# Two value products in a row: latent attention with its products done for a pair of items in every other step

## The reference, cut to what matters

```python
def _block_attention(q, k, v):          # 8 heads, 512 queries, 768 keys (256 context + 512 latent)
    ...
    def one(qi):                        # a block of 128 queries
        s = jnp.einsum('bqhd,bkhd->bhqk', qi, k, preferred_element_type=jnp.float32) * scale
        p = jax.nn.softmax(s, axis=-1).astype(v.dtype)
        return jnp.einsum('bhqk,bkhd->bqhd', p, v)
```

## Time and profile before

| | |
|---|---|
| median of 3 runs | 2680.9 us |
| profiled execution, time | 2680.16 us |
| its span | 2678.4 us |
| TensorE busy | 2626.2 us, 98% |
| VectorE busy | 1157.1 us, 43% |
| ScalarE busy | 924.9 us, 35% |
| the stretch of the 32 items, from the span's start | 472 to 577.4 us |
| TensorE busy from 490 to 570 us | 80.00 of 80 us |

### The profile page before, as it was taken

How to read it: one execution, slowest core, us unless ns; L and a number is a source line. 1 busy time by engine, 2 the same in 40 slices (tenths; PEclk the granted TensorE clock), 3 DMA queues, 4 the chain that set the end, 5 groups by cost and what they waited for, 6 DMA issues and landing times.

```text
span 2678.4 us, 34877 instructions
## 1 busy us (share of the span) xinstructions
PE 2626.2 (98%) x14767; PEld 2154.1 (80%) x14767; DVE 1157.1 (43%) x1737; ACT 924.9 (35%) x1401; POOL 157.4 (6%) x268
## 2 busy tenths in 40 slices
PE   7999999999999999999999999999999999999998
PEld 5888887678888888867888888888888776888887
DVE  3414653666333243567433324333234467533322
ACT  3222333643222234455322223222224456322211
POOL 0140000001000001111000000000000010100000
PEclk9999999999999999999999999999999999999999
DMA  9631241012333332211233332333233212232221
GB/s 296 211 128 48 64 126 40 33 56 79 95 94 96 108 100 79 64 48 64 95 95 96 105 113 66 125 95 95 94 95 99 64 48 80 71 95 95 94 96 78
DMA packets 213953, 249.12 MB, mean 93 GB/s; under 512 B 12880, under 2 KB 193703, under 8 KB 213799
## 3 DMA queue, kind: packets, MB, share of 16 engines
q1 hardware_dynamic: 213798, 246.90, 28.9%
HBM read 244.78 MB, written 2.10 MB: 92 GB/s over the span
## 4 chain that ended last, share of the span: by engine, by line
PE 92%; DVE 3%; ACT 2%; issue 1%; POOL 1%; DMA 0%; SPq 0%; DVEq 0%; POOLq 0%; ACTq 0%
PE psum L751 89%; PE psum L1293 1%; PE psum L1209 1%; PE psum L821 1%; DMA mod_w<-in_ab_w_mod 0%; DVE stats_first L2021 0%; DVE work L2014 0%; DVE w_lo L1934 0%; ACT w_hi L1467 0%; POOL stats_first L2604 0%; DVE X L2017 0%; ACT work L1508 0%; ACT log_weights L1485 0%; POOL stats L2659 0%; DVE wide L2047 0%
## 5 line engine op out<-in xcount | busy, mean ns | idle before, releaser
L751 PE MATMUL psum<-h_hi,w_hi 128*128 128x512 f32 (+1 forms) x2096 | 782.7, 373 | 0.6 <-DVE w_lo L1934 0.3
L751 PE MATMUL psum<-h_lo,w_hi 128*128 128x512 f32 (+1 forms) x2096 | 775.6, 370 | 0.0
L751 PE MATMUL psum<-h_hi,w_lo 128*128 128x512 f32 (+1 forms) x2096 | 775.5, 370 | 0.0
L1934 DVE TENSOR_TENSOR w_lo<-raw,w_hi 128x2048 fp32r<-128x2048 f32 (+1 forms) x174 | 396.8, 2283 | 695.7 <-ACT w_hi L1467 695.6
L751 PEld LDWEIGHTS psum<-h_hi,w_hi 128*128 128x128 f32 x2096 | 395.9, 189 | 76.0 <-issue 8.4
L751 PEld LDWEIGHTS psum<-h_hi,w_lo 128*128 128x128 f32 x2096 | 395.3, 189 | 67.9
L751 PEld LDWEIGHTS psum<-h_lo,w_hi 128*128 128x128 f32 x2096 | 395.7, 189 | 64.7 <-issue 0.5
L1467 ACT ACTIVATE w_hi<-raw 128x2048 fp32r<-128x2048 f32 (+1 forms) x174 | 329.3, 1894 | 236.1 <-PE psum L751 230.3
L751 PE MATMUL psum<-w_hi,ff_hi 128*128 128x512 f32 x576 | 224.6, 390 | 0.0
L751 PE MATMUL psum<-w_lo,ff_hi 128*128 128x512 f32 x576 | 224.1, 389 | 0.0
L751 PE MATMUL psum<-w_hi,ff_lo 128*128 128x512 f32 x576 | 224.1, 389 | 0.0
(11 more groups left out here) (313 smaller groups left out, 3143.7 us busy)
## 6 DMA issues: line engine op xcount, KB each, us to landing
raw<-in_ffn_w_gate SPq DMA_DIRECT2D x44, 1024.0 KB, 5.3
raw<-in_ffn_w_up SPq DMA_DIRECT2D x44, 1024.0 KB, 5.3
raw<-in_ffn_w_down SPq DMA_DIRECT2D x44, 1024.0 KB, 4.8
raw<-in_w_in SPq DMA_DIRECT2D x36, 512.0 KB, 5.2
raw<-in_ab_w_in SPq DMA_DIRECT2D x10, 1024.0 KB, 8.0
mod_w<-in_ab_w_mod SPq DMA_DIRECT2D x8, 1024.0 KB, 12.0
raw<-in_w_out SPq DMA_DIRECT2D x8, 1024.0 KB, 4.8
raw<-in_cd_w_in SPq DMA_DIRECT2D x7, 1024.0 KB, 5.9
```

The lines of the kernel that those rows point to most:

```text
L751: return pe.matmul(o, lhsT, rhs, start=start, stop=stop, skip_group_check=True)
L1934: dve.tensor_tensor(lo[:, 0:nk * n], raw[c % 2][:, 0:nk * n], hi[:, 0:nk * n].bitcast(F32), ALU.subtract).then_inc(*w_lo_made.mark(key))
```

## The change

The value products leave the even steps. In every odd step from 3 on, TensorE does those of items n - 3 and n - 2 one after the other, behind the scores of item n and the turns of item n - 1. VectorE's scalings of the two items go to the same place of its program. ScalarE's program, the DMA queue's and GpSimd's stay as they are, and no instruction is added or dropped.

```diff
-                if 0 <= n - 2 < len(seq):
-                    hd, t = seq[n - 2]
+                for m_ in (n - 3, n - 2) if n % 2 and n > 2 else ():
+                    hd, t = seq[m_]
                     b = claim(rot.take(), ("pv", hd, t))
-                    if n == 2:
+                    if m_ == 0:
                         pe.wait_ge(*v_made[5])
                     pe.wait_ge(*probs_turned["mla", hd, t])
                     pe.wait_ge(*turned_dve["mla", hd, t])
                     for k in range(6):
                         for p0 in (0, 64):
-                            m = mm(psum[p0:p0 + 64, b * BANK:b * BANK + 64], probsT[(n - 2) % 2][:, k * P + p0:k * P + p0 + 64],
+                            m = mm(psum[p0:p0 + 64, b * BANK:b * BANK + 64], probsT[m_ % 2][:, k * P + p0:k * P + p0 + 64],
                                    v_all[:, k, hd * 64:(hd + 1) * 64], k == 0, k == 5)
                     done(m, ("pv", hd, t))
...
-                if 0 <= n - 2 < len(seq):
-                    hd, t = seq[n - 2]
+                for m_ in (n - 3, n - 2) if n % 2 and n > 2 else ():
+                    hd, t = seq[m_]
                     event = ("pv", hd, t)
                     dve.wait_ge(*summed["mla", hd, t])
                     dve.wait_ge(*psum_full[event])
-                    dve.tensor_scalar(o_mla[:, t, hd * 64:(hd + 1) * 64], full(event, 64), stat("mla", n - 2, 3, 4), None,
+                    dve.tensor_scalar(o_mla[:, t, hd * 64:(hd + 1) * 64], full(event, 64), stat("mla", m_, 3, 4), None,
                                       ALU.mult).then_inc(*attn_put.mark(("mla", hd, t)))
```

## The result

The changed kernel takes 2685.02 us, the median of 20 runs (2683.69 to 2686.57), against 2680.4 us before (20 runs, 2679.29 to 2681.83). The ratio is 1.0017, 95% interval 1.0011 to 1.0022: slower by 4.6 us. That is under the 0.2% of the prediction, though with this many runs the interval lies clear of 1. The forecast was 2685.0.

A forecast was written before the change was run, and what follows sets the result against it. TensorE, busy 98%, sets the pace. Waits +9.90, tile changes -5.25, last wait -1.00 and step 22 +0.4 make +4.1 us: 2684.3, plus 0.7 for the runs' median, 2685.0 us; range 2682.5 to 2688.5, the mechanism's own 2683.5 to 2686.5.

The forecast's parts named there:

- The uncovered path: TensorE waits for the exponential of each even item from 2 to 30: 15 waits of 0.66 us, +9.90 us.
- The changes of tile saved: Value products on TensorE stand in 15 blocks less, each saving 0.35 us of tiling-mode changes: -5.25 us.
- The last wait: TensorE's idle time before the last item's turns, 0.97 us plus the restart, goes: -1.00 us.
- Item 22: VectorE's maximum in step 22 starts 0.42 us late behind query copies and a weight piece: about +0.4 us.
- The step within a pair: From one value product to the next on TensorE: bounds 0 and 0.16 us per new pair, taken as 0.
- The sum: All terms over the stretch together: 9.90 - 5.25 - 1.00 + 0.4 = +4.1 us.
- The hidden wait (1): Rival: TensorE's wait stays hidden, only the savings remain, about -6.2 us, 2674.7 us; 4 in 100.
- (2): Rival: the 0.35 us belongs to each value product, not the change of tile; +9.4 us, 2690.3 us; 8 in 100.
- (3): Rival: VectorE becomes late in odd steps, two scalings ahead of the next maximum; +1.8 us, 2686.8 us; 6 in 100.
- (4): Rival: the step within a pair costs near its upper bound; +6.5 us in all, 2687.4 us; 6 in 100.
- waits in even steps: TensorE waits for the exponential in every other step, about 0.6 us each; turns there without idle time would refute the forecast.
- Its last sign of being wrong: VectorE's maximum beginning later than 0.2 us behind its scores in more steps than 22 would refute the forecast.

The follow-up runs named there:

- Experiment 1: Row maximum of latent attention taken over 128 of 768 columns, in both kernels: kernel before 2679.24 us (ratio 0.9997), changed kernel 2675.21 us (0.9979).
- Experiment 2: Value products on the whole array, 6 in place of 12, in both kernels: kernel before 2689.53 us (ratio 1.0035), changed kernel 2701.39 us (1.0075).
- experiment 5: Changed kernel with VectorE's copies of the queries' turned part in steps 4, 12, 20 instead of 5, 13, 21: 2684.16 us, ratio 1.0012.

## Why the prediction was right

Point by point, against the intervals of the trace after:
- **The uncovered path.** 2.57 us from an item's scores to its turns, 1.94 of cover, 0.66 with the restart: measured 2.58 for 14 of the 15 even items from 2 to 30. Experiment 1 takes the wait away and finds the cover itself, 1.95.
- **The changes of tile saved.** 0.35 us each: two steps came to 2.58 + 3.72 = 6.30 us against 6.29 reckoned and 5.98 before. Experiment 2 shows that a pair saves nothing where the products stay on the whole array. How the 0.35 is shared out was only partly right, since 0.06 of the 0.10 in the scores stays on the whole array.
- **The last wait.** -1.00: it is gone, and the last turns begin 2.58 + 2.33 = 4.91 us behind item 29's, for 4.90 reckoned. The interval before them fell only from 2.58 to 2.33 because a whole value product (0.70) moved into it.
- **Item 22** (the prediction's step 22). 0.42 late, +0.4 net: shown in the trace after and in experiment 5.
- **The step within a pair.** Taken as 0 between bounds of 0 and 0.16: measured 0.
- **The sum.** +4.1 in the stretch: measured +4.10 between the profiled executions, +4.6 between the medians of 20 runs. The stretch ends at 582.45 and not near 581.5, since it began 0.9 later. That the median of 2685.02 falls on the 2685.0 forecast is luck: the forecast started from 2680.9, the median of 3 runs, where 20 runs give 2680.4, and the step is larger by as much.
- **The rivals.** The hidden wait (1) is refuted by 15 waits; that the 0.35 belongs to each product (2) by the pair's 1.55 us; among even items VectorE was late for item 22 alone, against (3); (4) by the same 1.55.

Some details of the forecast did not hold. The waits view prints 8.5 us for TensorE, not some 10, since it reckons from modelled ends. And where the forecast speaks of waits in even steps, it means even items: their turns stand in the odd step that follows. Its last sign of being wrong, a maximum later than 0.2 us behind its scores in more steps than 22, did show in 11 odd steps (0.33 behind, 0.74 in step 23); it was worded too widely, since the maxima of odd items have slack, and the time was not touched. The pair is new in 15 places, not 14 (15 x 0.16 is the 2.4 that it gives). And the forecast's own range of 2683.5 to 2686.5 holds the 1.5 of the waits alone, without the 0.7 that it also names.

That the 0.35 us is a drain of the array, as the Trainium skill says of changing the tiling mode ("TensorEngine Tiling (Array Packing)", Tiling Modes), was not measured as such; the runs show that it comes and goes with the half-array products, all but 0.06 of it in the scores.

## What to carry to other kernels

Before moving work on the busiest engine, read the path from a stage's end to the next stage that needs it, where nothing hides it (the last item shows it), and hold it against what is left between them in the new order. Here work taken out of a cover cost nothing as long as the cover was longer than the path (2.99 against 2.57 us), and from there on one for one (0.64 for a cover of 1.94, 0.41 more where the path was 0.42 longer). If grouping like work pays, put the group where it covers the path of every item, and then look for the next thing it waits for: here a copy that stood behind an exponential and could as well go ahead of it.

## What the hardware showed that I had not expected

Turns right behind value products on the half array take 0.71 us, and 0.65 otherwise; scores in that place take 1.39 against 1.29. Scores behind whole-array value products still take 1.35, and two such products 2.62 us, again 0.06 over twice 1.28. So part of the cost sits in whatever comes next, and not all of it has to do with the shape; why, no run tells. And six products on the whole array take 1.28 us where twelve on two halves take 0.85 with their opening and closing, 1.55 for 2.62 in a pair. With all its changes of shape a step on the half tiles takes 2.99 us, for 3.29 on the whole array: they are worth it.
